# Sums of two products in one product of 512 columns, their halves joined on VectorE, and mends at the joints between stages

## The reference, cut to what matters

```python
xn = rmsnorm(h, mix_norm_g[l])
proj = xn @ w_in[l]
u_conv, qkv, q_mem, gates = jnp.split(proj, SPLITS, axis=-1)
y_conv = conv_module(u_conv, conv_w[l], conv_b[l], conv_ln_g[l], conv_ln_b[l]) @ w_conv_out[l]
...
g = jax.nn.sigmoid(gates + gate_b[l]).reshape(b, s, N_BRANCH, d)
merged = g[:, :, 0] * y_conv + g[:, :, 1] * y_attn + g[:, :, 2] * y_mem
h = h + merged @ w_o[l]
hn = rmsnorm(h, ffn_norm_g[l])
up = causal_dwconv(hn @ w_up[l], ffn_conv_w[l], ffn_conv_b[l])
```

## Time and profile before

| what | value |
|---|---|
| median of three runs | 3058.36 us (3047.41 to 3058.36) |
| the profiled execution, time and span | 3047.6 us, 3045.8 us |
| PE busy | 2971.7 us (98%) |
| DVE, ACT, POOL busy | 2092.2 us (69%), 1460.3 us (48%), 182.8 us (6%) |
| share of the chain that ended last | PE 88%, DVE 6%, ACT 3% |
| w_lo on DVE (L1679) | 534, mean 2301 ns |
| w_hi on ACT (L587) | 534, mean 1911 ns |

### The profile page before, as it was taken

The page is one execution under the profiler, slowest core; times in us unless marked ns, Lnnn a source line. Parts: engine busy times, 40 slices in busy tenths (PEclk is TensorE's granted clock), DMA queues, the critical chain, the costliest instruction groups (busy, mean ns, idle before and its releaser), DMA issues.

```text
span 3045.8 us, 53542 instructions
## 1 busy us (share of the span) xinstructions
PE 2971.7 (98%) x21856; PEld 2820.6 (93%) x21856; DVE 2092.2 (69%) x2403; ACT 1460.3 (48%) x1608; POOL 182.8 (6%) x254
## 2 busy tenths in 40 slices
PE   8999999999999999999999999999899999999997
PEld 8899899999999999999999989988889889889887
DVE  5543458887765789888888883455664885775874
ACT  5443553434444444444444443444544664564663
POOL 2000000000001000000000160111110000000001
PEclk9999999999999999999999989999999999999999
DMA  7545545554553787887887764443405896795881
GB/s 259 178 155 176 174 152 180 184 186 153 208 189 118 305 328 309 325 325 313 318 325 305 279 196 169 142 148 136 144 32 197 303 372 228 296 345 217 332 317 73
DMA packets 114824, 692.44 MB, mean 227 GB/s; under 512 B 14144, under 2 KB 27696, under 8 KB 33648
## 3 DMA queue, kind: packets, MB, share of 16 engines
q1 hardware_dynamic: 108512, 673.24, 59.1%
q10 hardware_dynamic: 5264, 13.11, 1.4%
q0 software_dynamic: 896, 3.93, 0.4%
HBM read 679.74 MB, written 10.49 MB: 227 GB/s over the span
## 4 chain that ended last, share of the span: by engine, by line
PE 88%; DVE 6%; ACT 3%; issue 1%; DMA 1%; POOL 0%; SPq 0%; DVEq 0%; ACTq 0%; POOLq 0%
PE psT L1089 18%; PE psT L1090 18%; PE psT L1091 18%; PE psT L1563 3%; PE psT L1565 3%; PE psT L1564 3%; PE psT L1552 2%; PE psT L1554 2%; PE psT L1553 2%; DVE w_lo L1679 2%; PE psY L1602 1%; PE psY L1603 1%; PE psY L1604 1%; PE psY L1240 1%; ACT w_hi L587 1%
## 5 line engine op out<-in xcount | busy, mean ns | idle before, releaser
L1679 DVE TENSOR_TENSOR w_lo<-raw,w_hi 128x2048 fp32r<-128x2048 f32 x534 | 1227.1, 2301 | 545.9 <-ACT w_hi L587 541.6
L587 ACT ACTIVATE w_hi<-raw 128x2048 fp32r<-128x2048 f32 x534 | 1020.1, 1911 | 536.9 <-DMA raw<-tiles_dram 188.4
L1089 PE MATMUL psT<-a_hi,w_hi 128*128 128x256 f32 x4240 | 1216.5, 287 | 29.0 <-DVE w_lo L1679 6.5
L1090 PE MATMUL psT<-a_lo,w_hi 128*128 128x256 f32 x4240 | 1205.4, 284 | 0.0
L1091 PE MATMUL psT<-a_hi,w_lo 128*128 128x256 f32 x4240 | 1205.0, 284 | 0.0
L1089 PEld LDWEIGHTS psT<-a_hi,w_hi 128*128 128x128 f32 x4240 | 819.8, 193 | 37.5 <-issue 19.3
L1090 PEld LDWEIGHTS psT<-a_lo,w_hi 128*128 128x128 f32 x4240 | 819.8, 193 | 0.3
L1091 PEld LDWEIGHTS psT<-a_hi,w_lo 128*128 128x128 f32 x4240 | 819.3, 193 | 0.0
L1089 PE MATMUL psT<-h_hi,w_hi 128*128 128x256 f32 (+1 forms) x800 | 228.4, 286 | 4.5 <-DVE pool L1987 2.6
L1091 PE MATMUL psT<-h_hi,w_lo 128*128 128x256 f32 (+1 forms) x800 | 227.5, 284 | 0.0
L1090 PE MATMUL psT<-h_lo,w_hi 128*128 128x256 f32 (+1 forms) x800 | 227.4, 284 | 0.0
(11 more groups left out here) (330 smaller groups left out, 3613.4 us busy)
## 6 DMA issues: line engine op xcount, KB each, us to landing
raw<-tiles_dram SPq DMA_DIRECT2D x534, 1024.0 KB, 5.4
pool<-ada_tiles_dram SPq DMA_DIRECT2D x96, 1024.0 KB, 4.8
bias_rows_dram<-pool ACTq DMA_DIRECT2D x1, 8192.0 KB, 49.5
pool<-bias_rows_dram SPq DMA_DIRECT2D x40, 128.0 KB, 4.4
pool<-bias_rows_dram SPq DMA_DIRECT2D x40, 64.0 KB, 4.6
pool<-mem_dram ACTq DMA_DIRECT2D x4, 512.0 KB, 9.5
pool<-x_dram ACTq DMA_DIRECT2D x1, 2048.0 KB, 12.1
pool<-x_dram POOLq DMA_DIRECT2D x1, 2048.0 KB, 8.7
```

The costliest lines, as they stand in the source:

```text
L587: nc.scalar.activation(w_hi[:, t.k % SPL, :], raw[:, t.k % RAW, :], ACT.Copy).then_inc(hi_done, 1)
L1089: nc.tensor.matmul(ps_out, wh, x_hi, start=first, stop=False)
L1090: nc.tensor.matmul(ps_out, wh, x_lo, start=False, stop=False)
L1679: nc.vector.tensor_tensor(w_lo[:, t.k % SPL, :], raw[:, t.k % RAW, :], w_hi[:, t.k % SPL, :].bitcast(F32), ALU.subtract).then_inc(lo_done, 1)
```

## The change

Before, the two products of `w_hi` went one after the other into the same 256 columns. Now `a_hi` and `a_lo` are halves of one tensor `a_both`, and one product of 512 columns (`both`) writes w_hi by a_hi to columns 0 to 255 and w_hi by a_lo to columns 256 to 511; w_lo by a_hi is added to the first half. The two halves must then be added: ACT copies the lower sums to SBUF, and DVE adds the upper (`join`). This holds for 157 tiles of 16 chunks: qm, q, k, glu, gates, ya, ym, yc, wo, and the second block's 29 tiles named "rows". The first block's other stages and the experts keep `three`.

The rest:

- DVE's loop over the gates is written out, so its waits have constants.
- The layer norm's chunks and squares are added by POOL, with one ones' product each.
- The first four key tiles are emptied unscaled, and the memory's squares come behind its splits.
- Fewer idle products (30 for 40 at the start, none ahead of ya, wo and the fourth tile of two).
- The first two tiles behind four of the norms or merges are multiplied together chunk by chunk.
- `merged` is split while yc is multiplied, and its chunks are stored eight places on.
- POOL no longer scales pairs: DVE does all, and the final norm's scaling of the first block moves to DVE, at tiles 18 to 33 of two.
- Small square roots (`warm_root`) are put ahead of where a root's table is wanted.
- The first loads of `load_ada` come behind tile loads.
- The routers' products and the transposes of the tokens alternate.

```diff
-        a_hi = sb("a_hi", [P, DC, S], F32R)
-        a_lo = sb("a_lo", [P, DC, S], F32R)
+        a_both = sb("a_both", [P, 2, DC, S], F32R)
+        a_hi, a_lo = a_both[:, 0, :, :], a_both[:, 1, :, :]
...
             sp.wait_ge(W["act_lo_ready"], split_end("ffn"))
-            for j in range(3):
-                load_ada(j, j)
             f0 = BASE["ffn"]
             for f in range(4, 12):
                 load_tile(Tile(f0 + f))
-                if f >= 8:
-                    load_ada(f - 5, (f - 5) % 3)
+                if f < 11:
+                    load_ada(f - 4, (f - 4) % 3)
...
+            def both(dst, w, a, k, first, last):
+
+                slot = w.k % SPL
+                wh, wl = w_hi[:, slot, k * P:k * P + P], w_lo[:, slot, k * P:k * P + P]
+                nc.tensor.matmul(dst.rearrange("p (h s) -> p h s", h=2), wh, a_both[:, :, a, :], start=first, stop=False)
+                return nc.tensor.matmul(dst[:, 0:S], wl, a_hi[:, a, :], start=False, stop=last)
...
+            def wide_two(t, fresh, at=0):
+
+                begin(t)
+                wide_part(t, range(8), fresh, at)
+                begin(t + 1)
+                wide_part(t + 1, range(8), None, at)
+                for k in range(8, DC):
+                    for x in (t, t + 1):
+                        last = wide_part(x, [k], fresh, at)
...
-            for c in range(HC):
-                last = nc.tensor.matmul(psN, ones[:, :], cv[:, c, :], start=c == 0, stop=c == HC - 1)
-            last.then_inc(W["mean_sums"], 1)
+            nc.tensor.matmul(psN, ones[:, :], var[:, :], start=True, stop=True).then_inc(W["mean_sums"], 1)
...
+            def join(src, dst, scale):
+
+                nc.vector.scalar_tensor_tensor(dst, src, scale, dst, ALU.mult, ALU.add).then_inc(emptied["D"], 1)
...
-            with dve.Fori(0, 4) as i:
-                with step.loop(i, 2 * TAPS - 2, 4):
-                    for k in range(12):
-                        lo(Tile(BASE["gates"] + k, i, 12) + AHEAD)
+            for i in range(4):
+                for k in range(12):
+                    n = 12 * i + k
+                    t = Tile(BASE["gates"] + n)
+                    lo(t + AHEAD)
...
+                    dve.wait_ge(W["lower_copied"], 5 * HC + n + 1)
+                    gate = pool[:, gate_slot(n), :]
+                    nc.vector.tensor_tensor(gate, psT[:, t.k % 2, 0:S], gate, ALU.add).then_inc(emptied["D"], 1)
```

More of the change, by code:

```diff
@@ L812, in _ @@
                 square("lnvar", g, CV, SQLN)
-            others("ya", 4, 4)
+            for k in range(4, HC):
+                lower_pair("ya", k)
             std("lnvar")
@@ L901, in _ @@
             std("final")
+            split(Tile(BASE["two"] + 2))
             act.wait_ge(used, BASE["two"])
@@ L954, in _ @@
                 attend(SECOND_UNITS, 20, SC2, ticks_at(n, 0, N_UNITS + 3))
-                if kind in ("rows", "tokens"):
+                if kind == "rows":
+                    act.wait_ge(used, t.count())
+                    nc.scalar.activation(pool[:, dest, :], psT[:, SLOT2[n], S:2 * S], ACT.Copy, scale=x)\
+                        .then_inc(W["lower_copied"], 1)
+                elif kind == "tokens":
                     act.wait_ge(used, t.count())
@@ L1421, in second_half @@
                         pe.wait_ge(emptied[who], OWN[:BASE["two"] + before + 1].count(who))
+                if n < 2:
+                    if n == half == 0:
+                        pe.wait_ge(lo_done, (t + 1).count())
+                        for k in range(DC):
+                            chunk_split("norm1", k)
+                            for m in range(2):
+                                last = both(psT[:, SLOT2[m], 0:2 * S], t + m, k, k, k == 0, k == DC - 1)
+                                if k == DC - 1:
+                                    last.then_inc(used, 1)
+                    return
                 if kind == "rows":
                     for k in range(8 * half, 8 * half + 8):
-                        chunk_split("norm1" if n == 0 else None, k)
-                        last = three(psT[:, slot, 0:S], t, a_hi[:, k, :], a_lo[:, k, :], k, k == 0, k == DC - 1)
+                        last = both(psT[:, slot, 0:2 * S], t, k, k, k == 0, k == DC - 1)
                 elif kind == "cmp":
@@ L2155, in _ @@
                 if n == 1:
-                    dve.wait_ge(emptied["A"], OWN[:BASE["two"] + 1].count("A"))
+                    dve.wait_ge(emptied["D"], OWN[:BASE["two"] + 1].count("D"))
                     cmp_in(0)
@@ L2159, in _ @@
                     cmp_lo(0)
-                    dve.wait_ge(emptied["A"], OWN[:BASE["two"] + 2].count("A"))
+                    dve.wait_ge(emptied["D"], OWN[:BASE["two"] + 2].count("D"))
                     cmp_in(1)
@@ L2370, in lanes @@
                     lane_group(g, sq, lane, "lanes_added")
-            def odd_pairs(name, src, rows):
-                for p in range(1, 8, 2):
-                    pair = chunks(src + 2 * p, 2)
-                    nc.gpsimd.tensor_tensor(pair, pair, rows.unsqueeze(1).to_broadcast([P, 2, S]), ALU.mult)\
-                        .then_inc(W["normed_odd"], 1)
             pl.dma_start(sinks, sinks_d.partition_broadcast(P)).then_inc(L["sinks"], 16)
```

467 lines of the change are left out of this document (304 added, 163 removed).

## The result

The changed kernel takes 3015.9 us (median of 4 runs, 3010.2 to 3019.7) for 3056.8 us before in the same session. The ratio is 0.9871, with a 95% interval from 0.9844 to 0.9898. The profiled execution took 3018.2 us (span 3016.5) for 3047.6. It is faster, as forecast, but by some 40 us and not by 78: the time lies above my range, which ended at 3000. One execution of 12365 us of a later experiment (e6) is left out of its ratio.

What follows compares the result with a forecast made beforehand. PE was taken to bound the kernel, by little. Terms of 33.4 + 6.1 + 10 + 2.3 + 10 + 9 + 5 + 2 = 77.8 us off the profiled 3047.6 gave 2969.8, stated as 2970 us, range 2945 to 3000.

Steps and rivals of the forecast that it cites:

- rival 2: Gates: DVE becomes the bound, taps staying at 0.67 us, 6.01 us a tile; 2989 us in all, chance 10%.
- the joint ahead of wo: PE's 2.9 us away from tiles ahead of wo shrinks, as eight chunks are ready beforehand: 2.3 us saved.
- ffn: Entry of ffn: DVE alone scales pairs, 3.8 us won at the third tile, 6.3 at the fourth; 10 us, bounds 6 and 14.
- the experts' entry: Ahead of the experts: half the token turning done between router products, about 4.2 us, and 1 from the pairs; 5 us.
- the ones' products: Norms: one of eight products remains for the mean and one of eight for the variance, saving 6.1 us of PE.
- Rival 4: Wide products: the two-block operand is read at a worse rate, making the kernel slower, as far as 3254 us; chance 2%.
- Rival 1: Wide products: a joining saves only a fifth of 13.3 ns, the second block bringing back fixed cost; 2997 us, chance 8%.
- the wide products: In 157 tiles, 2512 pairs of 256 columns become one of 512, each saving 13.3 ns: 33.4 us.
- glu: The glu stage was to gain 3.4 us, its tiles leaving DVE more room for the join than the gates.
- The start: First key tiles: second tile begins at about 22.7 us, the third no longer waits for the norm; 10 us, bounds 5 and 12.
- Entry of two: Start of stage two: about eleven us won at the first pair, 4.6 given back at the third tile; 9 us, bounds 4 and 13.
- Rival 3: Joints give back half of 44 us, through PE at 1.2 GHz or the next wait taking over; 2989 us, chance 20%.

Runs made afterwards that it cites:

- e6: Changed kernel with ScalarE and VectorE reading a tile's sums in ya, ym and yc before splitting the tile three on; ratio 0.9873 to the kernel before.
- e1: Changed kernel with each 512-column product taken apart into two of 256, sums still joined on VectorE; 3033.5 us, ratio 0.9936 to the kernel before.
- e13: Changed kernel, operand in two blocks, with one to four idle products ahead of the gates' tiles in turn; 3034.0 us (one run).
- e14: Changed kernel with the operand in one block and one to four idle products ahead of the gates' tiles in turn; 3040.9 us (one run).
- e2: Changed kernel with the two parts of a chunk side by side, so the wide product reads one block; 3016.2 us, ratio 0.9882 to the kernel before.
- e5: Changed kernel with VectorE emptying each of the first four key tiles before splitting the tile three on; ratio 0.9868 to the kernel before.
- e7: Changed kernel with idle products put back or added where PE waits and a half-clock stretch follows; ratio 0.9861 to the kernel before.
- e4: Changed kernel with each of the two ones' products made eight times over; ratio 0.9884 to the kernel before.
- e10: Changed kernel with VectorE's attention step moved ahead of the join of glu; ratio 0.9872 to the kernel before.
- e16: Changed kernel with ScalarE's sigmoid of even glu tiles moved behind its attention step; ratio 0.9897 to the kernel before.

## Why the prediction was wrong in size

Right were the direction, the bound and several of the mechanisms: PE and not DVE bounds the gates, the taps come at 0.52 us (rival 2 is out, by the trace and by e1), the joint ahead of wo is gone (its first three tiles 17.95 us for 20.72, of which 0.6 is their products), ffn gave 9.2 of 10, the experts' entry 5.8 of 5, the end 1.9 of 2, the ones' products 3.2 us at each place. Rival 4 is out. Rival 1 is out as it stood: the second block costs nothing (e13 against e14), and a joining saves 6.7 or 13.3 ns, never a fifth. By the Trainium skill (TensorE: Matmul & The Clock Gate, Back-to-back issue gap) it would have been 2.5 ns, an estimate from its formula for an isolated product; the trace agrees at neither spacing.

ffn's total was right by luck in part. The first two tiles won 2.0 us of the 6.3 that I had, the third tile stood at 1.1 for 3.8, the fourth gave its 6.3, and 1.7 came at tile 163, which was not in my sum.

Two things failed. The larger is the sum of all that is not the wide products: 44.4 us forecast, 20 came by e1, since most places were priced down to the wait that goes and not to the next one. The other is the price of a joining. The sum had 77.8 us; between the two profiled executions lie 29.4. The 48 that lack, place by place:

1. **The wide products, 33.4 forecast, 20 by e1.** The step that failed is "Each joining saves 13.3 ns", taken from runs of equal products. A 512 followed by a 256 need not take the sum of what each takes among its like: at the slower spacing it is 6.7 ns more, in two of three tiles, some 11 us.
2. **glu, 3.4 forecast, -2.9 came.** "Their tiles leave DVE more room than the gates" looked at busy time; this stage hangs on a chain through DVE and ACT for the attention. PE waits for it 1.82 us at tile 53 and 1.47 at 61, where the kernel before had 0.55 and nothing. A stretch at half clock follows the first wait, but it isn't the cause: e2, e5 and e7 have none there and take 128.6. e1 has glu at 129.2 with the old products, so not the wide products but something in the rest of the change costs the 3 us. That it is the split way of emptying is likely, not shown; neither order that I turned was it. The 3.4 us forecast for this stage are part of the 13 that lack under point 1.
3. **The start, 10 forecast, 2.8 came.** "The second tile can begin at about 22.7" was right (it began at 22.88), and emptying unscaled did remove the wait for the norm. What took its place is the load of the tile three on, by the order of `key_tile`: 4 us by e5. The other 3 are not traced.
4. **ya and ym, 3.1 us.** I priced the ones' products that go, and not what they had covered: the emptying two tiles later (e4, e6). Spacing accounts for 1.4 more.
5. **Entry of two, 9 forecast, about 2 came.** Eleven us at the pair were 9.0, and the third tile gave 4.9 of them back (a wait of 3.2, and 1.7 at half clock), where I had 4.6. Tile 287 won 1.7. What I did not have is tile 289: 3.9 us longer, 1.6 of it a new wait for `h_lo` and the rest half clock. What makes `h_lo` late there was not tested.
6. **wout, 4.7.** Nowhere in my sum. Its waits of 2.2 to 2.9 us were there before; whether half clock follows one changes from kernel to kernel with the same code (none before and in e10, one in e1 and in e16, whose wout takes 127.0, three in the changed kernel). Each stretch costs 1.4 to 1.7 us.
7. **The experts, 4.5.** The 5.8 us of the entry were there, and were given back 130 us later, as loads came late (351 GB/s from 2400 to 2460 us). Over the kernels with this code unchanged the stage takes 760.5 to 768.4 us, in one profiled execution of each, so an effect of this size can't be told in it.

Rival 3 came nearest: the 44 gave back 24 by e1, a little more than the half that it had (half of 44 is 22, so its own time should have been 2992, not 2989). Its "next wait takes over" is what most of the places above show, each with a wait of its own, of which it named only the third tile of two. Its half clock had a small part: 85 us for 77 before, which is 4 us of time, though it fell anew in wout.

What stays open is what decides between the two spacings where PE starts again, which link holds glu, what makes `h_lo` late at tile 289, and whether the change costs the experts anything.

## What to carry to other kernels

Work that is taken off the engine that bounds the kernel is worth its price only down to the next wait: name, for each piece, what had been hidden under it (here an emptying two tiles on, a load three tiles on, and probably an attention's chain). In a queue, read what others wait for before starting work that itself waits for a load. Measure a spacing on the pattern that will run, not on its parts. Size idle products by the wait that they fill: where they outlast it, they cost what the clock gives back. Don't count gains of a few us ahead of a stage that runs at the pace of its loads.

## What the hardware showed that I had not expected

- A 512-column and a 256-column product in turn come at 0.3467 or 0.3533 us a pair, with the same instructions and full clock. Which of the two is taken up where PE starts again: in one loop two idle products always led to the faster and one, three or four to the slower, 11 times of 11, but elsewhere three came with the faster. In the gates the slower one's chunks start 0.35, 0.36 and 0.35 us apart in turn. In groups of two and two a tile is always 5.57 us, of eight and eight 5.59.
- A stretch of 3.4 us or more at the 1.2 GHz level (granted clock 0.5) followed waits of PE of 1.8 to 3.9 us in one kernel and not in the next, at the same wait: wout took 125.4 us with none and 130.1 with three.
- 40 us less at half clock (85 to 45) brought no gain that the timing can tell by itself. At four waits of 2.2 to 2.9 us, 14 idle products of 3.1 us cost 5.0 us in all, and the four stretches at half clock that they took away had cost 6.3.
